# Four column groups for the low-rank gate, full-row operands for the samples' recurrent step, output squares added on VectorE, 512-wide values and 128-key scores in a two-layer hybrid decoder

## The reference

```
q, k, v, g_lr, r = split(h @ w_in)                    # g_lr has 16 columns
log_a = log_sigmoid(g_lr @ w_g2 + b) / 16             # gate from a low rank of 16
S_t = diag(a_t) S_{t-1} + k_t^T v_t ;  o_t = q_t S_t  # exact, in chunks
y = (rms_per_head(o) * silu(r)) @ w_out
```

## Time and profile before

| | |
|---|---|
| median of 3 runs | 2367.81 us (2367.75 to 2571.14) |
| profiled execution, slowest core (5) | span 2366.8 us; the page gives no other time of it |
| spans of the 8 cores | 2353.9 to 2366.8 us |
| mean granted TensorE clock | 0.992 to 0.995 of full |
| PE busy | 2308.5 us, 98% |
| DVE, ACT, POOL busy | 1224.0 us, 1171.9 us, 316.9 us (52%, 50%, 13%) |
| transfers written to the core | 357.11 MB, mean 151 GB/s |

### The profile page before, as it was taken

The page is one execution under the profiler, slowest core; times in us unless marked ns, Lnnn a source line. Parts: engine busy times, 40 slices in busy tenths (PEclk is TensorE's granted clock), DMA queues, the critical chain, the costliest instruction groups (busy, mean ns, idle before and its releaser), DMA issues.

```text
span 2366.8 us, 42650 instructions; the slowest of 8 cores (2353.9 to 2366.8 us)
## 1 busy us (share of the span) xinstructions
PE 2308.5 (98%) x14660; PEld 1130.0 (48%) x14660; DVE 1224.0 (52%) x2180; ACT 1171.9 (50%) x2316; POOL 316.9 (13%) x598
## 2 busy tenths in 40 slices
PE   5999999999999999999999899999999999999999
PEld 2445545554445444445444355454444444544444
DVE  4535674466434566456443355644664355644742
ACT  4634655554643465554552156555555335644541
POOL 1111111111111111110111111111111111011010
PEclk9999999999999999999999899999999999999999
DMA  9997798888997999977999988888899999598793
GB/s 171 176 167 129 143 156 136 130 138 146 160 154 126 179 158 159 174 131 144 183 157 173 172 133 141 138 141 144 154 157 172 162 155 177 94 158 146 138 173 90
DMA packets 101362, 357.11 MB, mean 151 GB/s; under 512 B 12528, under 2 KB 17440, under 8 KB 101024
## 3 DMA queue, kind: packets, MB, share of 16 engines
q0 software_dynamic: 84032, 326.13, 83.3%
q1 hardware_dynamic: 17120, 28.25, 3.9%
HBM read 662.94 MB, written 15.40 MB: 287 GB/s over the span
## 4 chain that ended last, share of the span: by engine, by line
PE 94%; DMA 4%; issue 1%; DVE 1%; ACT 0%; SPq 0%; ACTq 0%; DVEq 0%; POOLq 0%
PE pst L617 90%; DMA ring<-wfi 2%; DMA ring<-wfo 1%; DMA x<-xp 1%; PE pst L1412 1%; PE pst L1351 1%; DMA ring<-wqd 1%; PE pst L1373 0%; PE pst L989 0%; PE pst L972 0%; PE pst L990 0%; PE pst L1377 0%; PE pst L1435 0%; DVE h L633 0%; ACT pb L622 0%
## 5 line engine op out<-in xcount | busy, mean ns | idle before, releaser
L617 PE MATMUL pst<-h,ring 128*128 128x512 bf16 x6144 | 1382.8, 380 | 4.3 <-DVE h L633 3.1
L617 PEld LDWEIGHTS pst<-h,ring 128*128 128x128 bf16 x6144 | 589.9, 98 | 701.4 <-issue 27.6
L617 PE MATMUL pst<-r,ring 128*128 128x512 bf16 x3136 | 711.6, 382 | 8.6 <-DMA ring<-wfo 8.6
L622 ACT ACTIVATE pb<-pb 128x512 f32<-128x512 f32 x856 | 535.0, 629 | 66.4 <-DVE pb L825 7.8
L622 ACT ACTIVATE pb<-pst 128x512 f32<-128x512 f32 (+1 forms) x472 | 278.5, 595 | 447.2 <-PE pst L617 440.0
L630 DVE TENSOR_TENSOR pb<-pb,pst 128x512 f32<-128x512 f32 x368 | 252.0, 686 | 452.4 <-ACT pb L622 448.9
L617 PEld LDWEIGHTS pst<-r,ring 128*128 128x128 bf16 x3136 | 303.0, 98 | 368.6 <-issue 19.0
L513 POOL DMA_DIRECT2D ring<-wfi x336 | 177.4, 529 | 1101.3 <-PE pst L617 1000.3
L622 ACT ACTIVATE h<-x 128x512 bf16<-128x512 f32 x192 | 119.0, 627 | 364.3 <-DVE x L633 270.5
L630 DVE TENSOR_TENSOR r<-pb,pst 128x512 bf16<-128x512 f32 x336 | 230.5, 687 | 46.3 <-DVE pb L630 39.1
L633 DVE SCALAR_TENSOR_TENSOR x<-pst,x 128x512 f32<-128x512 f32 x128 | 88.3, 690 | 219.1 <-PE pst L617 218.7
(11 more groups left out here) (150 smaller groups left out, 1098.2 us busy)
## 6 DMA issues: line engine op xcount, KB each, us to landing
ring<-wfi POOLq DMA_DIRECT2D x336, 512.0 KB, 8.5
ring<-wfo POOLq DMA_DIRECT2D x128, 672.0 KB, 8.3
ring<-wgl POOLq DMA_DIRECT2D x64, 512.0 KB, 7.0
x<-xp SPq DMA_DIRECT2D x16, 512.0 KB, 11.5
y_p<-x SPq DMA_DIRECT2D x32, 256.0 KB, 8.0
ring<-wqd POOLq DMA_DIRECT2D x12, 512.0 KB, 12.5
ring<-wod POOLq DMA_DIRECT2D x16, 384.0 KB, 9.1
ring<-wkv POOLq DMA_DIRECT2D x8, 512.0 KB, 7.6
```

What stands on the lines that cost most here:

```text
L617: ins = e.matmul(out, lhsT=l, rhs=r, start=(start and i == 0), stop=(stop and i == last), skip_group_check=skip)
L622: return O(ACT, lambda e: e.activation(out=out, in_=in_, func=func, scale=scale, bias=bias), reads, writes, c_act(n))
```

## The change

The low rank is computed in two calls of four matmuls, each matmul writing its own 32 partitions, so that four partial sums stand below one another. The second factor is stored four times (rows 16 to 31 of each copy zero), and the gate's matmul sums the partial results over 128 rows. The samples' values, masked keys and score block are read as 128 rows, of which the last 96 are zero; a memset of the scratch at the start makes them so. A `v` unit now holds half the contraction for two heads instead of the whole for one, and matmuls for values are 512 wide. Squares of the two halves are added on DVE before one matmul sums them. `block2` computes scores on 128 keys for tiles 1 to 3 and uses the first `nk` of them.

```diff
-    WLR = A("WLR", [128, 8, 16], BF16)
-    WG2 = A("WG2", [16, 512], BF16)
+    WLR = A("WLR", [128, 8, 32], BF16)
+    WG2 = A("WG2", [128, 512], BF16)
...
+    def lowrank(T, b):
+        n = T.n
+        hn = T.hn
+        for q in range(2):
+            kts = range(4 * q, 4 * q + 4)
+            yield need(lambda: all(("h", T.nm, hn, kt) in done for kt in kts))
+            def fw(e):
+                ins = None
+                for g in range(4):
+                    ins = e.matmul(PS[b][32 * g:32 * g + 32, 0:n], lhsT=WLR[:, 4 * q + g, :], rhs=T.h[:, 4 * q + g, :], start=(q == 0), stop=(q == 1))
+                return ins
+            yield O(PE, fw, [hk(T, kt) for kt in kts] + ["WLR"], [("ps", b)], 0.1 + c_mm(1, n))
...  gla and gla_s
-        yield from mmh(T, (PS[b][0:16, :],), lambda kt, z: WLR[:, kt, :], ["WLR"], (b,), n)
+        yield from lowrank(T, b)
-        yield copy(ACT, glr, PS[b][0:16, :], n, [("ps", b)], [gk])
+        yield copy(ACT, glr, PS[b], n, [("ps", b)], [gk])
-                yield mm(PS[b], [(WG2[0:16, hd * 128:(hd + 1) * 128], glr)], [gk, "WG2"], b, n)
+                yield mm(PS[b], [(WG2[:, hd * 128:(hd + 1) * 128], glr)], [gk, "WG2"], b, n)
...  gla, values
-        for hd in range(4):
-            u = yield from use(T, "v", hd)
-            for cp in range(2):
-                for a in range(2):
-                    yield mm(PS[b][:, a * 256:(a + 1) * 256], [(T.h[:, kt, c * 128:(c + 1) * 128], v[:, kt, :]) for kt in range(8)], h8 + [u.key], b, 256)
+        for hp in range(2):
+            us = []
+            for z in range(2):
+                us.append((yield from use(T, "v", 2 * hp + z)))
+            for c in range(4):
+                for z in range(2):
+                    yield mm(PS[b], [(T.h[:, kt, c * 128:(c + 1) * 128], vs[z][:, kt % 4, :]) for kt in range(4 * z, 4 * z + 4)], h8 + [us[z].key], b, 512,
+                             start=(z == 0), stop=(z == 1))
...  rmsq
+            yield tt(s4[:, :, 0, :], s4[:, :, 0, :], s4[:, :, 1, :], ALU.add, 512, [pool.key(q)], [pool.key(q)])
-            yield mm(PS[b], [(ones, s4[:, :, f, :]) for f in range(2)], [pool.key(q), "CB"], b, n)
+            yield mm(PS[b], [(ones, s4[:, :, 0, :])], [pool.key(q), "CB"], b, n)
...  gla_s
-        vv = KA[0:32, 0:1024]
-        kms = KB[0:32, 384:896].rearrange("p (h w) -> p h w", h=4)
-        am = KB[0:32, 896:1024].rearrange("p (h w) -> p h w", h=4)
+        vv = KA[:, 0:1024]
+        kms = KB[:, 384:896].rearrange("p (h w) -> p h w", h=4)
+        am = KB[:, 896:1024].rearrange("p (h w) -> p h w", h=4)
-            yield mm(PS[b][0:32, 0:256], [(T.h[:, kt, :], v[:, kt, :]) for kt in range(8)], h8 + [u.key], b, 256)
+            yield mm(PS[b][0:32, :], [(T.h[:, kt, :], vs[kt // 4][:, kt % 4, :]) for kt in range(8)], h8 + [u.key for u in us], b, 512)
-            yield O(PE, fo, [gk, ub.key] + gv, [("ps", b)], 1.68)
+            yield O(PE, fo, [gk, ub.key] + gv, [("ps", b)], c_mm(16, 8))
...  block2
+            np_ = 128 if t else 32
-                            ins = e.matmul(PS[bs[hp]][0:nk, rr * 64 + jj * 32:rr * 64 + jj * 32 + 32],
-                                           lhsT=KT[hp * 64:hp * 64 + 64, jj, sl_(r, nk, 16)],
+                            ins = e.matmul(PS[bs[hp]][0:np_, rr * 64 + jj * 32:rr * 64 + jj * 32 + 32],
+                                           lhsT=KT[hp * 64:hp * 64 + 64, jj, sl_(r, np_, 16)],
-                    [("ps", b) for b in bs], 16 * (0.029 + nk * 0.00027))
+                    [("ps", b) for b in bs], 16 * 0.05)
...  prologue
+        yield O(PL, lambda e: e.memset(KT[:, :, 512:2048], 0.0), [],
+                [rk(TS, k) for k in ["g", "go", "kms"] + [("gv", h) for h in range(4)]], 2.4)
```

More of the change, by code:

```diff
@@ L589, in build @@
     ACTK = [("act", j) for j in range(NF)]
-    CELLK = [("cq", h) for h in range(4)] + [("ck", h) for h in range(4)] + [("cv", h, c) for h in range(4) for c in range(2)] \
+    CELLK = [("cq", h) for h in range(4)] + [("ck", h) for h in range(4)] + [("cv", h, c) for h in range(2) for c in range(4)] \
         + [("o", h) for h in range(4)] + [("u", m) for m in range(8)] + [("ktok", h) for h in range(4)] + [("am", k) for k in range(4)]
@@ L807, in gla @@
         (b,) = yield from get_banks(1)
-        yield from mmh(T, (PS[b][0:16, :],), lambda kt, z: WLR[:, kt, :], ["WLR"], (b,), n)
+        yield from lowrank(T, b)
         (gi,) = yield from pool.get("glr", 1, 1)
-        glr, gk = pool.aps[gi][0:16, 0:256].bitcast(BF16), pool.key(gi)
-        yield copy(ACT, glr, PS[b][0:16, :], n, [("ps", b)], [gk])
+        glr, gk = pool.aps[gi][:, 0:256].bitcast(BF16), pool.key(gi)
+        yield copy(ACT, glr, PS[b], n, [("ps", b)], [gk])
         put(b)
@@ L833, in gla, with vpost @@
         TH.spawn(gate(), -5, T.rank)
-        def vpost(hd, cp, b, eng):
-            yield copy(eng, T.cell[:, hd, 2 * cp:2 * cp + 2, 256:512], PS[b].rearrange("p (c w) -> p c w", c=2), n, [("ps", b)], [rk(T, ("cv", hd, cp))])
+        def vpost(hp, c, b, eng):
+            yield copy(eng, T.cell[:, 2 * hp:2 * hp + 2, c, 256:512], PS[b].rearrange("p (a w) -> p a w", a=2), n, [("ps", b)], [rk(T, ("cv", hp, c))])
             put(b)
-        for hd in range(4):
-            u = yield from use(T, "v", hd)
-            v = u.ap.rearrange("p (kt c) -> p kt c", kt=8)
-            for cp in range(2):
-                (b,) = yield from get_banks(1)
-                for a in range(2):
-                    c = 2 * cp + a
-                    yield mm(PS[b][:, a * 256:(a + 1) * 256], [(T.h[:, kt, c * 128:(c + 1) * 128], v[:, kt, :]) for kt in range(8)], h8 + [u.key], b, 256)
-                TH.spawn(vpost(hd, cp, b, either()), -3, T.rank)
-            u.left -= 1
+        for hp in range(2):
+            us = []
+            for z in range(2):
+                us.append((yield from use(T, "v", 2 * hp + z)))
+            vs = [u.ap.rearrange("p (kt c) -> p kt c", kt=4) for u in us]
+            for c in range(4):
+                (b,) = yield from get_banks(1)
+                for z in range(2):
+                    yield mm(PS[b], [(T.h[:, kt, c * 128:(c + 1) * 128], vs[z][:, kt % 4, :]) for kt in range(4 * z, 4 * z + 4)], h8 + [us[z].key], b, 512,
+                             start=(z == 0), stop=(z == 1))
+                TH.spawn(vpost(hp, c, b, either()), -3, T.rank)
+            for u in us:
+                u.left -= 1
         def qkpost(hd, bs):
@@ L973, in fk @@
                 return ins
-            yield O(PE, fk, [rk(T, ("ktok", hd)) for hd in hs] + [rk(T, ("cv", hd, c // 2)) for hd in hs], [("ps", bk)], c_mm(2, 256))
+            yield O(PE, fk, [rk(T, ("ktok", hd)) for hd in hs] + [rk(T, ("cv", hp, c))], [("ps", bk)], c_mm(2, 256))
             for a, hd in enumerate(hs):
@@ L991, in fo @@
                 return ins
-            yield O(PE, fo, [rk(T, ("am", k)), ("Sbf", hp)] + [rk(T, ("cv", hd, c // 2)) for hd in hs] + [rk(T, ("cq", hd)) for hd in hs],
+            yield O(PE, fo, [rk(T, ("am", k)), ("Sbf", hp)] + [rk(T, ("cv", hp, c))] + [rk(T, ("cq", hd)) for hd in hs],
                     [("ps", bo)], c_mm(8, 128))
@@ L997, in recur @@
             yield copy(ACT, T.of[:, hs[0]:hs[1] + 1, c, :, :].rearrange("p a f w -> p a (f w)"), PS[bo].rearrange("p (a w) -> p a w", a=2), 512,
-                       [("ps", bo)], [rk(T, ("o", hd)) for hd in hs] + [rk(T, ("cv", hd, c // 2)) for hd in hs]
+                       [("ps", bo)], [rk(T, ("o", hd)) for hd in hs] + [rk(T, ("cv", hp, c))]
                        + [rk(T, ("cq", hd)) for hd in hs] + [rk(T, ("ck", hd)) for hd in hs])
@@ L1031, in gla_s @@
         (b,) = yield from get_banks(1)
-        yield from mmh(T, (PS[b][0:16, 0:n],), lambda kt, z: WLR[:, kt, :], ["WLR"], (b,), n)
-        glr = KB[0:16, 896:928]
-        yield copy(ACT, glr, PS[b][0:16, 0:n], n, [("ps", b)], [gk])
+        yield from lowrank(T, b)
+        glr = KB[:, 1024:1056]
+        yield copy(ACT, glr, PS[b][:, 0:n], n, [("ps", b)], [gk])
         put(b)
@@ L1040, in fg @@
             for hd in range(4):
-                ins = e.matmul(PS[b][:, hd * n:(hd + 1) * n], lhsT=WG2[0:16, hd * 128:(hd + 1) * 128], rhs=glr, start=True, stop=True)
+                ins = e.matmul(PS[b][:, hd * n:(hd + 1) * n], lhsT=WG2[:, hd * 128:(hd + 1) * 128], rhs=glr, start=True, stop=True)
             return ins
@@ L1052, in gla_s @@
         yield act(C4, C4, AF.Exp, 128, pk_, pk_, scale=1.0 / 16)
-        for hd in range(4):
-            u = yield from use(T, "v", hd)
-            v = u.ap.rearrange("p (kt c) -> p kt c", kt=8)
+        for hp in range(2):
+            us = []
+            for z in range(2):
+                us.append((yield from use(T, "v", 2 * hp + z)))
+            vs = [u.ap.rearrange("p (kt c) -> p kt c", kt=4) for u in us]
             (b,) = yield from get_banks(1)
-            yield mm(PS[b][0:32, 0:256], [(T.h[:, kt, :], v[:, kt, :]) for kt in range(8)], h8 + [u.key], b, 256)
-            u.left -= 1
```

(33 more changed lines are left out.)

4 lines of the change are left out of this document (2 added, 2 removed).

## The result

| | before | after |
|---|---|---|
| median, us | 2368.43 (4 runs) | 2339.47 (4 runs, 2338.16 to 2343.13) |
| ratio, 95% interval | | 0.988 [0.9868, 0.9893] |
| span of the profiled execution, slowest core, us | 2366.8 | 2339.0 |
| PE busy / idle in it, us | 2308.5 / 58.3 | 2277.9 / 61.1 |
| spans of the 8 cores, us | 2353.9 to 2366.8 | 2325.4 to 2339.0 |

The kernel became 1.2% faster, 29 us, less than the 2% bound and more than its own interval. The forecast was 2343.4 (24.4 us), the range 2332 to 2359.

The account below looks back on a forecast made before the run. PE, busy 98% of the span, was taken to bound the kernel, so savings in its stream come off the end. The terms summed to 24.4 us: 2367.8 - 24.4 = 2343.4 us, range 2332 to 2359.

Parts of the forecast that it names:

- low rank and gate: Prompt tiles and samples: four low-rank matmuls stream nearly together, 5.0 + 0.1 us; gate matmuls on 128 rows lose switches, 3.2 + 0.2.
- samples' step and state update: Samples' recurrent mixer: matmuls on 128 rows instead of 32 save 4.9 us in four calls, 1.6 in the state updates.
- scores, matmul time: Attention of tiles 1 and 2: scores on 128 keys are cheaper than on 64 or 96, 4.3 us saved.
- scores, clock: Tile 1's attention: rival that denser scores keep the clock up, another 5.0 us, giving 2338; chance 0.12.
- squares: Output squares added on DVE: 16 matmuls of 512 columns go from PE, 3.5 us saved.
- addition on DVE: 16 additions of squares, 6.7 us on DVE, covered by the other tile's feed-forward: no cost; uncovered, 6.7 us.
- values 512 wide: Prompt tiles' value matmuls: 64 of 512 columns instead of 128 of 256 a tile, 1.7 us saved.
- samples' values: Samples' values in two calls instead of four lose four switches, 0.4 us saved.
- start: Kernel start: the memset costs nothing, the larger gate tables delay the first weights, 0.5 us lost.
- switch of 0.10 us: PE's stream: entering or leaving a form that uses less of the array costs about 0.10 us each.
- Late weights: Feed-forward: rival that another work order brings one more weight stall, 10.6 us, giving 2354; chance 0.15.
- slower rival: Mixer stage of each tile: value units held in pairs delay the next landing, at most 56 us, giving 2399; chance 0.05.

Follow-up runs that it names:

- the order experiments: Kernel before with the change's two modelled costs, 5.7 us slower; changed kernel with both old costs, the step's or the scores': +2.2, +2.0, +0.7 us.

## Why the prediction was right, point by point

| term | predicted, us | measured, us | by |
|---|---|---|---|
| low rank and gate | 5.0 + 0.1 + 3.2 + 0.2 = 8.5 | 9.1 | undone |
| samples' step and state update | 4.9 + 1.6 = 6.5 | 7.4 | undone |
| scores, matmul time | 4.3 | 3.0 to 4.3 | undone, alone |
| scores, clock | rival, 5.0 | 3.0 to 3.2 | undone, alone |
| squares | 3.5 | 3.2 | undone |
| addition on DVE | 0 | -0.7, within the spread | nearly left out |
| values 512 wide | 1.7 | -0.2 | undone |
| samples' values | 0.4 | not tried | |
| start | -0.5 | not tried alone | |

**What bounds the kernel** held: PE's stream sets the time, so what was taken from it came off the end. The measured parts come to 9.1 + 7.4 + 6.2 + 3.2 - 0.7 - 0.2 = 25.0 of 28.9 us. The rest, about 4 us, was not taken apart, and its size is itself uncertain: with each difference taken to before on the same chip, the same parts come to 9.7 + 8.0 + 6.2 + 3.8 + 1.2 + 0.4 = 29.3, and nothing is left. The samples' values, the start and another order of all the work were not tried alone, and the order experiments moved the time by as much as the rest.

**The switch of 0.10 us** was the right unit: it is at both ends of the 32-row forms, present and absent at will with the order fixed. The Trainium skill says that changing the tiling mode drains the engine ("TensorEngine Tiling (Array Packing)", Key Properties). The traces agree in that the changes of form measured here cost time, 0.10 us each.

**The low rank.** Nearly full overlap, 4 x 0.216 in 0.23 us, is 3.7 times. The 3.07 of the Trainium skill that I weighed ("TensorE: Matmul & The Clock Gate", Measured speedup vs the span model) is stated for four row groups; four column groups did better here.

**The samples' step** was mis-sized on the safe side: I took 35 ns a matmul and it was 25, so a call fell by 1.39 and not 1.23 us, 0.6 us in all. The Trainium skill ("TensorE: Matmul & The Clock Gate", Back-to-back issue gap) has about 25 ns as the least distance of two small matmuls and 62 ns only with hardware decode off; the trace agrees with the 25, and the 62 that I weighed did not bind.

**The scores.** The matmul time came as read from the row of tile 3. What the sum lacked is the clock: I gave it a chance of 0.12 and 5.0 us as a case for itself, while 3 us of it come with the scores. Before showed the sign, half clock right behind tile 1's scores, and I argued against it that the new ones were small as well. Even so tile 1 was not the place that the experiments bear out; tile 2 was. The 100, 62 and 44 ns at 96, 64 and 128 keys follow the weight loads. The Trainium skill says that fast weight load asks for 128 columns of weights ("TensorE: Matmul & The Clock Gate", Weight-path perf modes), and these numbers fit that; no run here shows the load mode itself.

**How much of the agreement is luck.** The median came out 3.9 us under the forecast and 1.5 above the 2338 of the clock case. Without the clock's 4.5 us the gain is 24.4, the very sum that was forecast, and that is partly luck: the parts that were tried give 9.1 + 7.4 + 3.0 + 3.2 - 0.7 - 0.2 = 21.8 us without the clock, where their terms said 24.5. The other 2.6 us come from what was not tried alone, where the terms said -0.1.

**Values 512 wide** is the term that failed. The row of 640 matmuls mixed 512 value matmuls with 128 of the shared values; in after those 128 alone cost 15.6/128 = 122 ns, so they had raised the mean of 115.8. A difference of 6.5 ns between two means of different company was no price.

**Late weights and the slower rival.** The longest stall for weights, 8.6 us, is still there with 8.3, and the next longest for `wfi` is 2.5 us, so no new one was bought. The pairs of units cost PE 0.2 us.

## What to carry to other kernels

In a kernel whose matrix engine never rests, count the changes of array form in its stream before its columns: a matmul with 16 or 32 rows costs 0.2 us more than a zero-padded one of 128 when it stands alone. In a run of small matmuls, give weights of 64 or 96 columns 128 even where the extra results are thrown away (weights of 32 columns gain nothing: tile 0's scores cost 2.8/64 = 44 ns as well), and pack narrow outputs in column groups. Take a price from start-to-start times in one context, not from the mean of a group that mixes several, and look at the granted clock behind every run of small matmuls.

## What the runs showed of the hardware that I had not expected

The clock fell to half with PE counted as busy throughout: on core 5 with the 96-key scores it was 0.50 from 2007 to 2019 us with no idle time, where the 128-key scores left it at 1.00 in that attention. Wide scores are no guarantee: with the squares in two matmuls, all scores of tiles 1 to 3 on 128 keys, core 4 was at 0.50 from 1072 to 1076 us, behind 48 of tile 1's with a wait of 0.49 us among them. And more weight columns can load faster than fewer: one load lasts 161 ns at 128 keys against 271 at 96, and a score matmul takes 44 ns against 100.
